# Layer norms computed in place in PSUM, with ScalarE's squares for the variance, and another order of work at the start of the forgetting attention

## The reference

```python
def layer_norm(x, g, b):
    mu = jnp.mean(xf, axis=-1, keepdims=True)
    var = jnp.mean(jnp.square(xf - mu), axis=-1, keepdims=True)
    y = (xf - mu) * lax.rsqrt(var + LN_EPS)
    return y * g + b
...
# forgetting attention
log_f = jax.nn.log_sigmoid(fl + b_f).transpose(0, 2, 1)
cum = jnp.cumsum(log_f, axis=-1)
logits = q @ k.T * scale + cum[:, :, s0:s1, None] - cum[:, :, None, :s1]
p = masked_softmax(logits, causal)
...
for i in range(DEPTH):
    x = layer_norm(ALPHA * x + mixer(x), ln1_g[i], ln1_b[i])
    x = layer_norm(ALPHA * x + conv_ffn(x, ...), ln2_g[i], ln2_b[i])
```

## Time and profile before

| | us |
|---|---|
| runs: median, lowest, highest of 3 | 1389.68, 1387.82, 1391.71 |
| profiled execution: its own time, its span | 1391.82, 1390.0 |
| PE, DVE, ACT, POOL busy | 1332.6, 666.7, 656.1, 604.5 |

### The profile page before, as it was taken

How to read it: one execution, slowest core, us unless ns; L and a number is a source line. 1 busy time by engine, 2 the same in 40 slices (tenths; PEclk the granted TensorE clock), 3 DMA queues, 4 the chain that set the end, 5 groups by cost and what they waited for, 6 DMA issues and landing times.

```text
span 1390.0 us, 19809 instructions
## 1 busy us (share of the span) xinstructions
PE 1332.6 (96%) x6858; PEld 1110.8 (80%) x6858; DVE 666.7 (48%) x1471; ACT 656.1 (47%) x1225; POOL 604.5 (43%) x398
## 2 busy tenths in 40 slices
PE   8979999989999999999999899998999999999997
PEld 6868887767888888888888788787788888888886
DVE  3347777774744334330017766768364433341006
ACT  4347677775344444441113767767244444443120
POOL 2267777653434444445434222222245444444441
PEclk9999999999999999999999999999999999999999
DMA  9442322223223333324232321222423333334321
GB/s 298 101 104 57 89 70 71 71 67 121 79 79 101 102 94 99 97 91 136 93 90 93 85 62 48 79 69 69 152 75 109 104 91 92 104 93 134 97 69 61
DMA packets 172798, 131.98 MB, mean 95 GB/s; under 512 B 24544, under 2 KB 156244, under 8 KB 172724
## 3 DMA queue, kind: packets, MB, share of 16 engines
q1 hardware_dynamic: 172724, 131.02, 32.3%
HBM read 117.17 MB, written 4.39 MB: 87 GB/s over the span
## 4 chain that ended last, share of the span: by engine, by line
PE 78%; DVE 10%; issue 4%; ACT 2%; DMA 2%; POOL 2%; SPq 2%; DVEq 0%; POOLq 0%; ACTq 0%
PE ps L955 15%; PE ps L956 15%; PE ps L957 15%; PE ps L1209 7%; PE ps L1212 7%; PE ps L1210 7%; PE ps L1115 2%; DVE xt L1639 2%; PE ps L1129 2%; PE ps L1082 2%; DVE ptl L1501 1%; DVE prob L1483 1%; SPq L343 1%; DVE xt L1629 1%; DVE stats L1633 1%
## 5 line engine op out<-in xcount | busy, mean ns | idle before, releaser
L487 POOL TENSOR_TENSOR wl<-raw,wh 128x1024 fp32r<-128x1024 f32 x178 | 432.5, 2433 | 659.0 <-ACT wh L609 658.9
L955 PE MATMUL ps<-xh,wh 128*128 128x512 f32 x968 | 382.8, 395 | 0.0
L957 PE MATMUL ps<-xh,wl 128*128 128x512 f32 x968 | 378.3, 391 | 0.0
L956 PE MATMUL ps<-xl,wh 128*128 128x512 f32 x968 | 378.2, 391 | 0.0
L609 ACT ACTIVATE wh<-raw 128x1024 fp32r<-128x1024 f32 x192 | 201.6, 1051 | 197.8 <-PE ps L1212 189.9
L957 PEld LDWEIGHTS ps<-xh,wl 128*128 128x128 f32 x968 | 182.2, 188 | 39.5
L955 PEld LDWEIGHTS ps<-xh,wh 128*128 128x128 f32 x968 | 182.5, 188 | 35.6 <-ACT qf L683 1.2
L956 PEld LDWEIGHTS ps<-xl,wh 128*128 128x128 f32 x968 | 182.5, 189 | 33.6
L1660 DVE SCALAR_TENSOR_TENSOR work<-ps,conv,work 128x511 f32<-128x511 f32 x88 | 65.9, 749 | 222.0 <-ACT work L838 156.2
L703 ACT ACTIVATE prob<-prob,negmax 128x128 f32<-128x128 f32 x192 | 107.4, 559 | 69.9 <-DVE negmax L1483 68.0
L1209 PE MATMUL ps<-wh,gh 128*128 128x512 f32 x352 | 139.1, 395 | 0.0
(11 more groups left out here) (196 smaller groups left out, 1968.5 us busy)
## 6 DMA issues: line engine op xcount, KB each, us to landing
raw<-in_ffn_w_up SPq DMA_DIRECT2D x88, 512.0 KB, 3.8
raw<-in_ffn_w_down SPq DMA_DIRECT2D x44, 512.0 KB, 3.5
raw<-in_fox_w_in SPq DMA_DIRECT2D x24, 512.0 KB, 4.0
raw<-in_nsa_w_in SPq DMA_DIRECT2D x12, 512.0 KB, 5.1
xt<-in_x SPq DMA_DIRECT2D x8, 512.0 KB, 5.1
raw<-in_nsa_w_in SPq DMA_DIRECT2D x16, 256.0 KB, 3.7
qs<-work SPq DMA_DIRECT2D x32, 128.0 KB, 2.3
raw<-in_nsa_w_o SPq DMA_DIRECT2D x8, 512.0 KB, 3.8
```

Source lines behind the costliest of these rows:

```text
L487: nc.gpsimd.tensor_tensor(wl[:, slot, :, :], raw[:, slot, :, :], wh[:, slot, :, :].bitcast(F32), ALU.subtract).then_inc(s_wl, 1)
L955: nc.tensor.matmul(o, ah, bh, start=start, stop=False)
L956: nc.tensor.matmul(o, ah, bl, start=False, stop=False)
L957: return nc.tensor.matmul(o, al, bh, start=False, stop=stop)
```

## The change

The residual sum is written back into the tile's PSUM banks, and each of its halves gives its row sum; DVE makes the negated mean from the two; ACT squares the tile out of PSUM with that mean as bias and gives the sum of squares, and takes the root of it. DVE makes the low part of tile m-1 before the gamma pass, which now waits for the squares and works in PSUM; the beta pass reads PSUM and writes `xt`. At the start of the forgetting attention Ln comes ahead of the query copies and the cumulated sum ahead of the queries' low part. The negation moves into the constant rows of `cstack` (POOL writes -1 and 1 in two memsets), so both negated copies go. At v = 0 the transposes of a unit's probabilities stand behind the `kstep` products.

```diff
-            sp.wait_ge(s_fd, 7)
-            sp.wait_ge(s_fm, 6)
+            sp.wait_ge(s_fd, 5)
+            sp.wait_ge(s_fm, 7)
...
-                    sp.dma_start(fqb[par][r0:r0 + 4, h, :].bitcast(F32), row[2:6, :]).then_inc(s_bl[par], 16)
-                    sp.dma_start(fkd[par][r0:r0 + 4, h, 1, :].bitcast(F32), row[0:4, :]).then_inc(s_bl[par], 16)
+                    sp.dma_start(fqb[par][r0:r0 + 4, h, :].bitcast(F32), row[0:4, :]).then_inc(s_bl[par], 16)
+                    sp.dma_start(fkd[par][r0:r0 + 4, h, 1, :].bitcast(F32), row[2:6, :]).then_inc(s_bl[par], 16)
...
-            nc.gpsimd.memset(cstack[0:HEADS, 2:4, :].bitcast(F32), 1.0).then_inc(s_fm, 1)
-            pool.wait_ge(s_fm, 6)
+            nc.gpsimd.memset(cstack[0:HEADS, 0:2, :].bitcast(F32), -1.0).then_inc(s_fm, 1)
+            nc.gpsimd.memset(cstack[0:HEADS, 4:6, :].bitcast(F32), 1.0).then_inc(s_fm, 1)
+            pool.wait_ge(s_fm, 7)
...
             def tile_std(n, m):
-                act.wait_ge(s_mv, QT * n + m + 1)
-                nc.scalar.activation(std[:, m:m + 1], moments[:, m, 1:2], ACT.Sqrt, bias=eps[:, 0:1]).then_inc(s_std, 1)
+                t0 = QT * n + m
+                act.wait_ge(s_mv, t0 + 1)
+                if t0:
+                    act.wait_ge(s_sq, t0)
+                nc.scalar.activation(swapped.bitcast(BF16), ps[:, 2 * m:2 * m + 2, :].rearrange("p h c -> p (h c)"), ACT.Square, bias=negmean[:, m:m + 1],
+                                     accum_out=squares[:, m:m + 1]).then_inc(s_sq, 1)
+                act.wait_ge(s_sq, t0 + 1)
+                nc.scalar.activation(std[:, m:m + 1], squares[:, m:m + 1], ACT.Sqrt, bias=eps[:, 0:1], scale=1.0 / D).then_inc(s_std, 1)
...
+            act.wait_ge(s_fd, 2)
+            nc.scalar.activation(fe[0:HEADS, :], fe[0:HEADS, :], ACT.Ln).then_inc(s_fa, 1)
             act.wait_ge(s_fm, 2)
             fox_q_hi(C_FOX, 0)
-            act.wait_ge(s_fd, 2)
-            nc.scalar.activation(fe[0:HEADS, :], fe[0:HEADS, :], ACT.Ln).then_inc(s_fa, 1)
-            fox_k_hi(C_FOX + 1, 0, 0)
             act.wait_ge(s_fd, 4)
             act.wait_ge(s_rs, 16 * QT)
-            nc.scalar.activation(cstack[0:HEADS, 4, :], fcum[0:HEADS, :], ACT.Copy).then_inc(s_fa, 1)
+            nc.scalar.activation(cstack[0:HEADS, 2, :], fcum[0:HEADS, :], ACT.Copy).then_inc(s_fa, 1)
+            fox_k_hi(C_FOX + 1, 0, 0)
             fox_k_hi(C_FOX + 1, 0, 1)
...
-                    if v == 0:
-                        turn(U + v, v % 4)
                     if more:
...
-                    if v:
-                        turn(U + v, v % 4)
+                    turn(U + v, v % 4)
...
-                        nc.vector.scalar_tensor_tensor(out=xt[:, m, cs], in0=xt[:, m, cs], scalar=ALPHA, in1=ps[:, 2 * m + h, :],
-                                                       op0=ALU.mult, op1=ALU.add).then_inc(s_z, 1)
-                    for h in range(2):
-                        dve.wait_ge(s_z, 2 * t0 + h + 1)
-                        nc.vector.bn_stats(stats[:, m, h, :], xt[:, m, h * 512:(h + 1) * 512]).then_inc(s_bn, 1)
-                    dve.wait_ge(s_bn, 2 * t0 + 2)
-                    nc.vector.bn_aggr(moments[:, m, :], stats[:, m, :, :]).then_inc(s_mv, 1)
+                        nc.vector.scalar_tensor_tensor(out=ps[:, 2 * m + h, :], in0=xt[:, m, cs], scalar=ALPHA, in1=ps[:, 2 * m + h, :],
+                                                       op0=ALU.mult, op1=ALU.add, accum_out=zsum[:, m, h:h + 1]).then_inc(s_z, 1)
+                    dve.wait_ge(s_z, 2 * t0 + 2)
+                    nc.vector.tensor_scalar(negmean[:, m:m + 1], zsum[:, m, 0:1], zsum[:, m, 1:2], -1.0 / D, ALU.add, ALU.mult).then_inc(s_mv, 1)
+                    if banks and m:
+                        tile_lo(n, m - 1, banks[m - 1])
                     if m == 0:
                         dve.wait_ge(s_gb, 32 * (n + 1))
-                    dve.wait_ge(s_mv, t0 + 1)
-                    nc.vector.scalar_tensor_tensor(out=xt[:, m, :], in0=xt[:, m, :], scalar=moments[:, m, 0:1], in1=g_row,
-                                                   op0=ALU.subtract, op1=ALU.mult).then_inc(s_gz, 1)
-                    if banks and m:
-                        tile_lo(n, m - 1, banks[m - 1])
+                    dve.wait_ge(s_sq, t0 + 1)
+                    z = ps[:, 2 * m:2 * m + 2, :].rearrange("p h c -> p (h c)")
+                    nc.vector.scalar_tensor_tensor(out=z, in0=z, scalar=negmean[:, m:m + 1], in1=g_row,
+                                                   op0=ALU.add, op1=ALU.mult).then_inc(s_gz, 1)
...
-                        nc.vector.scalar_tensor_tensor(out=xt[:, m, cs], in0=xt[:, m, cs], scalar=rstd[:, m:m + 1], in1=b_row[:, cs],
+                        nc.vector.scalar_tensor_tensor(out=xt[:, m, cs], in0=z[:, cs], scalar=rstd[:, m:m + 1], in1=b_row[:, cs],
                                                        op0=ALU.mult, op1=ALU.add).then_inc(s_y, 1)
...
-            fox_lo(0, 0, NSA_ITEMS)
             dve.wait_ge(s_fa, 3)
...
             nc.vector.tensor_tensor_scan(fcum[hs, :], fone[hs, :], fz[hs, :], 0.0, ALU.mult, ALU.add).then_inc(s_fd, 1)
+            fox_lo(0, 0, NSA_ITEMS)
+            dve.wait_ge(s_fa, 4)
+            dve.wait_ge(s_fd, 4)
+            nc.vector.tensor_tensor(cstack[hs, 3, :], fcum[hs, :], cstack[hs, 2, :].bitcast(F32), ALU.subtract).then_inc(s_fd, 1)
             dve.wait_ge(s_fm, 3)
             fox_lo(0, 1, NSA_ITEMS + 1)
-            dve.wait_ge(s_fa, 4)
-            dve.wait_ge(s_fd, 4)
-            nc.vector.tensor_tensor(cstack[hs, 5, :], fcum[hs, :], cstack[hs, 4, :].bitcast(F32), ALU.subtract).then_inc(s_fd, 1)
-            nc.vector.tensor_scalar(cstack[hs, 0, :], cstack[hs, 4, :].bitcast(F32), -1.0, None, ALU.mult).then_inc(s_fd, 1)
-            dve.wait_ge(s_fd, 5)
-            nc.vector.tensor_scalar(cstack[hs, 1, :], cstack[hs, 5, :].bitcast(F32), -1.0, None, ALU.mult).then_inc(s_fd, 1)
```

More of the change, by code:

```diff
@@ L108, in build_trunk @@
         bf = sb("bf", [HEADS, 1])
-        stats = sb("stats", [P, QT, 2, 6])
-        moments = sb("moments", [P, QT, 2])
+        zsum = sb("zsum", [P, QT, 2])
+        negmean = sb("negmean", [P, QT])
+        squares = sb("squares", [P, QT])
         std = sb("std", [P, QT])
@@ L271, in build_trunk @@
         s_z = sem("tile_sums")
-        s_bn = sem("tile_statistics")
-        s_mv = sem("tile_moments")
+        s_mv = sem("tile_mean")
+        s_sq = sem("tile_squares")
         s_std = sem("tile_std")
```

## The result

Before 1390.7 us (median of 4 runs, 1387.8 to 1395.8), after 1374.0 us (4 runs, 1372.3 to 1374.3): ratio 0.988, 95% interval 0.986 to 0.990. The forecast was 1381.1 us with a range of 1377.0 to 1387.0, so the kernel became faster as forecast but by twice as much, 16.7 us for 8.6. The profiled execution took 1374.3 us, its span 1372.5.

What follows compares the result with a forecast made beforehand. The prediction took TensorE (PE), busy 1332.6 of 1390.0 us, as the bound. Terms -5.2 + 0.25 - 1.3 - 2.3 = -8.6 us from the runs' median of 1389.7 gave 1381.1 us, range 1377.0 to 1387.0.

Steps and rivals of the forecast that it cites:

- its first: Whole kernel: PE busy 1332.6 of 1390.0 us, its work left alone, so only some 57 us can be won.
- Inner norms: Three inner layer norms: PE's waits for tiles 2 and 3 go, tile 0 adds 0.0; gain 5.2 us.
- rival 3: Layer norms: Square and Sqrt don't share ACT's table, each tile loads twice; +9.4 us, 1399.1 us; chance 0.06.
- estimate of 1.2 us more: Norm passes: a PSUM source costs DVE 0.065 us more, 0.2 us a tile; left out of the sum.
- seven exposed tiles: Layer norms, 4 + 3 exposed tiles: PSUM writes at their dear end, +0.2 us a tile, add 1.4 us.
- ACT's square, feared for tile 3: Inner norms: tile 3's square queues behind tile 2's xh copies; 1.2 us of cover left before PE arrives.
- Last norm: Last layer norm: DVE becomes the bound of all four tiles, +0.09 us each; +0.25 us in all.
- Lead-in: Start of the forgetting attention: gate's DMA 2.3 us sooner, first maximum then straight behind L1702; gain 1.3 us.
- rival 2: First scores keep the full clock and pairs win more than 0.38 us: 1378.6 us; chance 0.10.
- The moved transpose: Forgetting attention, pairs 1 to 6: products wait only for ACT's value copy; 0.38 us six times, 2.3 us.

Runs made afterwards that it cites:

- e1_shift: Kernel before with one unused 128-byte tile behind bf, so every later tile starts 128 bytes further on: 1382.9 us beside 1390.6, ratio 0.9946.
- e2_after_shift: Changed kernel with the same unused 128 bytes, putting gh, gl and later tiles back on their addresses of before: 1382.3 us, ratio 0.9943.
- e4_lead: Kernel before with only the forgetting attention's other lead-in, later tiles on the addresses of before: 1388.6 us, ratio 0.9991.
- e5_turn: Kernel before with only the transpose of a unit's probabilities moved in the forgetting attention's loop, addresses of before: 1389.1 us, ratio 0.9984.

## Why the prediction was wrong, step by step

**The step that failed** is its first: "only some 57 us can be won by anything that leaves its work alone, as this change does". The change doesn't leave PE's work alone. It replaces small tiles by smaller ones, and every tile behind them moves by 128 bytes; 7.7 of the 16.7 us come from that (e1_shift; e2_after_shift from the other side). No step of the sum had a place for it, nor had a rival. Without it the change is worth 8.3 us (6.1 to 9.9 by its interval), the sum said 8.6, and 1382.3 us lies in the range. That the two are so near is in part luck, since the terms below were each mis-sized, in both directions.

**Inner norms**, forecast -5.2. The stretch beside POOL is gone as said, 1.29 and 1.28 us everywhere, no table load between tiles (rival 3 is out; Square at 1.12 + 0.20 us reads within its bounds), PSUM as source no dearer: 1.284 us for 1024 columns in L1652 against 1.28 before. The prediction's estimate of 1.2 us more, worked out from the Trainium skill (VectorE: DVE Perf Modes, The TRN2 errata), is not borne out (at its 0.2 us a tile its own seven exposed tiles would even make 1.4). A norm's two waits, for tiles 2 and 3, went, and one of 0.42 us came, for tile 0, where the chain is 3.01 us in the place of 2.84. Still the gain is 2.0 us a norm and not 1.72: between starts, tile 2's wait gave 0.36 where the wait's row shows 0.20, tile 3's 1.75 where it shows 1.52, and tile 0 cost 0.15. ACT's square, feared for tile 3, held nothing up. Total -6.0: the term was 0.8 too small.

**Last norm**, forecast +0.25, measured +0.6: the accumulator read takes 0.14 us and not 0.08 as the maximum's, the row it was sized by, so DVE's tile is 5.71 and not 5.66.

**Lead-in**, forecast -1.3. DVE became the next bound, the first maximum straight behind the values' sum, 1.3 us in e4_lead: mechanism and size. But together with the norms it is 2.9, since the clock is kept; the forecast had this as rival 2 with 0.10, and it is in both traces of the changed kernel. Of it 0.5 is lost again in the first pair, where a scaling of 2.2 us beside POOL now comes onto the path; it is back in the three kernels whose scaling is not stretched. Nothing in the forecast had that.

**The moved transpose**, forecast -2.3 at 0.38 a pair. The products stand 0.65 us in place of the transpose's 1.10, and from start to start a pair gains 0.5: -3.0. In the last pair 1.3 is given back through the clock in three traces (both of the changed kernel and e5_turn), which nothing in the forecast had.

So the terms, as the traces of the parts have them, are -6.0 + 0.6 - 2.9 + 0.5 - 3.0 + 1.3 = -9.5 us, and with the addresses' 6.7 -16.2. The two traces of the changed kernel have -16.2 and -16.1 from the first norm on. The trace of e2_after_shift, which keeps the clock in the last pair and so lacks the +1.3, has -10.8, as the terms say. Its timed runs say 8.3 and at most 9.9, a microsecond less; that difference stays open.

## What to carry to other kernels

Before a sum is made for a change that adds, removes or resizes a buffer, list what addresses move, and which matmuls have an operand among them: here 128 bytes were worth nearly as much as the whole work on norms and waits. Look at the pitch of a bound engine's repeated instruction in both traces before any wait is explained. A DVE scaling whose mean is four times its undisturbed time is an offer: one more operand took it off GpSimd's way and gave 4 to 6 us in the timed runs and 4.9 in the traces.

## What was not expected of the hardware

The pitch of these fp32r matmuls with 512 columns depends on the distance of stationary and moving operand modulo 256 bytes: 0.2267 us at 0, 0.228 to 0.230 at 64, 0.2325 at 128 in the down products, at the full granted clock and with PE busy throughout. Why isn't shown, and no other distance was tried. Whether a DVE scaling of 0.28 us takes 2.5 us beside POOL hangs on 0.02 us between their starts, and 2 us of the kernel's time with it. The same stand of PE of 1.44 us at the start of the forgetting attention is followed by the full granted clock in eight traces and by half of it for some 3 us in three; what else decides is open. A VectorE accumulator read takes 0.14 us behind a scalar_tensor_tensor and 0.08 behind the maximum and the scaling.
